# First block's mixing stage: the four q tiles first, the values between the k tiles; and the positions asked for before the bias tables

## The reference, cut to what matters

```python
h = _rmsnorm(x, mix_pre_g[l])
proj = h @ w_in[l]
qa, ka, va, qb, kb, vb, gate_a, gate_b = jnp.split(proj, splits, axis=-1)
ya = _neighbourhood_attention(qa.reshape(ha), ka.reshape(ha), va.reshape(ha), na_rpb[l]) @ w_branch_a[l]
...
s = jnp.einsum('brqhd,brkwhd->bhrqkw', qg, kg).astype(jnp.float32) * ATTN_SCALE
s = s + bias[None].astype(jnp.float32)
```

```python
inv_freq = jnp.power(jnp.float32(ROPE_THETA), -jnp.arange(0, dim, 2, dtype=jnp.float32) / dim)
ang = positions.astype(jnp.float32)[..., None] * inv_freq
```

## Time and profile before

| | |
|---|---|
| median of 3 runs | 3240.6 us (3239.19 to 3242.43) |
| the profiled execution's own time | 3239.51 us |
| its span in the profile | 3237.6 us |
| PE (TensorE matmul) busy | 3097.5 us, 96% of the span, 15386 matmuls |
| DVE busy | 1713.5 us, 53% |
| ACT busy | 1200.4 us, 37% |
| POOL busy | 292.5 us, 9% |
| mean TensorE clock granted | 0.986 of full |
| DMA | 339.65 MB, mean 105 GB/s |

### The profile page before, as it was taken

The page is one execution under the profiler, slowest core; times in us unless marked ns, Lnnn a source line. Parts: engine busy times, 40 slices in busy tenths (PEclk is TensorE's granted clock), DMA queues, the critical chain, the costliest instruction groups (busy, mean ns, idle before and its releaser), DMA issues.

```text
span 3237.6 us, 40494 instructions
## 1 busy us (share of the span) xinstructions
PE 3097.5 (96%) x15386; PEld 2514.2 (78%) x15386; DVE 1713.5 (53%) x3078; ACT 1200.4 (37%) x2229; POOL 292.5 (9%) x351
## 2 busy tenths in 40 slices
PE   7999989999999998999999999999999899999997
PEld 5888777788788887777768888887777767888886
DVE  5653354446555326655656555435656665555434
ACT  3322334443423233644542323223545453332222
POOL 2000110001100001111001100012111001100002
PEclk9999999999999998999999999999999999999998
DMA  4333373225232332224216222333323314323332
GB/s 148 109 98 115 99 143 111 92 88 175 86 104 93 115 98 71 96 88 149 74 40 189 97 98 92 102 106 117 94 85 107 126 43 146 124 92 103 95 96 91
DMA packets 107569, 339.65 MB, mean 105 GB/s; under 512 B 16608, under 2 KB 17136, under 8 KB 107248
## 3 DMA queue, kind: packets, MB, share of 16 engines
q1 hardware_dynamic: 86384, 273.90, 26.9%
q0 software_dynamic: 20992, 63.15, 6.5%
HBM read 300.55 MB, written 27.52 MB: 101 GB/s over the span
## 4 chain that ended last, share of the span: by engine, by line
PE 82%; ACT 6%; DVE 5%; issue 4%; DMA 2%; POOL 1%; SPq 0%; POOLq 0%; DVEq 0%; ACTq 0%
PE bk L1540 24%; PE bk L1542 24%; PE bk L1541 24%; ACT t L1760 2%; PE bk L1627 2%; PE bk L1605 2%; PE bk L1613 2%; PE bk L1577 1%; PE bk L1578 1%; PE bk L1579 1%; ACT t L1708 1%; ACT t L1768 1%; DVE t L1834 1%; PE bk L1590 1%; DMA t<-t 0%
## 5 line engine op out<-in xcount | busy, mean ns | idle before, releaser
L1540 PE MATMUL bk<-t,t 128*128 128x512 f32 x3808 | 1498.8, 394 | 67.9 <-DVE t L1834 27.1
L1542 PE MATMUL bk<-t,t 128*128 128x512 f32 x3808 | 1484.0, 390 | 0.0
L1541 PE MATMUL bk<-t,t 128*128 128x512 f32 x3808 | 1483.2, 389 | 0.0
L1540 PEld LDWEIGHTS bk<-t,t 128*128 128x128 f32 x3808 | 721.0, 189 | 239.1 <-issue 44.6
L1834 DVE TENSOR_TENSOR t<-t,t 128x1024 fp32r<-128x1024 f32 (+3 forms) x540 | 620.4, 1167 | 416.9 <-ACT t L1708 416.2
L1542 PEld LDWEIGHTS bk<-t,t 128*128 128x128 f32 x3808 | 720.4, 189 | 149.7
L1541 PEld LDWEIGHTS bk<-t,t 128*128 128x128 f32 x3808 | 721.5, 189 | 146.4 <-issue 1.7
L1708 ACT CAST t<-t 128x1024 fp32r<-128x1024 f32 (+3 forms) x540 | 513.5, 980 | 232.4 <-PE bk L1542 119.5
L1760 ACT ACTIVATE t<-t,t 128x256 f32<-128x256 f32 (+3 forms) x336 | 173.2, 516 | 140.8 <-DVE t L1911 140.0
L1751 ACT CAST t<-t 128x512 fp32r<-128x512 f32 x88 | 54.6, 621 | 441.7 <-DVE t L1898 441.7
L2141 POOL TENSOR_TENSOR t<-t,t 128x512 f32<-128x512 f32 x65 | 86.9, 1337 | 1428.9 <-ACT t L1738 1428.1
(11 more groups left out here) (165 smaller groups left out, 2035.1 us busy)
## 6 DMA issues: line engine op xcount, KB each, us to landing
t<-in_f_g SPq DMA_DIRECT2D x88, 512.0 KB, 4.3
t<-in_f_u SPq DMA_DIRECT2D x88, 512.0 KB, 3.6
t<-in_f_d SPq DMA_DIRECT2D x64, 512.0 KB, 4.4
t<-in_gate SPq DMA_DIRECT2D x48, 512.0 KB, 3.9
gate_scratch<-t POOLq DMA_DIRECT2D x64, 256.0 KB, 2.3
t<-gate_scratch POOLq DMA_DIRECT2D x64, 256.0 KB, 3.8
t<-in_f_d SPq DMA_DIRECT2D x32, 384.0 KB, 3.2
t<-in_wo SPq DMA_DIRECT2D x24, 512.0 KB, 3.8
```

Of the source, the lines that this page charges most:

```text
L1540: pe.matmul(o, wh, xh, start=start, stop=False)
L1541: pe.matmul(o, wh, xl, start=False, stop=False)
L1542: return pe.matmul(o, wl, xh, start=False, stop=stop)
```

## The change

Two edits. In the mixing stage the four q tiles are made first, in one `dense4` step; then k0 and k1; then the values with their store and their loads; then k2 and k3. In `rope_tables()` the load of the positions stands before the call of `bias_tables()`.

```diff
-        v_n = self.tokens_first("va", 512, 2, H, lambda t: vn[:, t, :], fr, by=lambda: (self.nv, self.nv_tok))
-        vst = self.load(D["values"].rearrange("(t p) c -> p t c", p=128), vn[:], v_n)
-        v_t = [[self.load(va[w][:, j, :],
-                          bass.AP(D["values"].tensor, (256 * j + WINDOWS[w]) * T, [[64 * T, 4], [T, 32], [1, T]]), fr, vst)
-                for j in range(2)] for w in range(4)]
         qt_, kt_ = [], []
         bt_ = {}
...
+        for m, r in enumerate(self.dense4([("qka", m) for m in range(4)], H)):
+            qt_.append(self.evacuate(OB, *r, qa[:, m, :].rearrange("p (t r c) -> p t r c", t=4, r=8), fr, view=by_columns))
         for m in range(4):
-            qt_.append(self.project("qka", m, H, qa[:, m, :].rearrange("p (t r c) -> p t r c", t=4, r=8), fr, view=by_columns))
-        for m in range(4):
+            if m == 2:
+                v_n = self.tokens_first("va", 512, 2, H, lambda t: vn[:, t, :], fr, by=lambda: (self.nv, self.nv_tok))
+                vst = self.load(D["values"].rearrange("(t p) c -> p t c", p=128), vn[:], v_n)
+                v_t = [[self.load(va[w][:, j, :],
+                                  bass.AP(D["values"].tensor, (256 * j + WINDOWS[w]) * T, [[64 * T, 4], [T, 32], [1, T]]),
+                                  fr, vst) for j in range(2)] for w in range(4)]
             kt_.append(self.project("qka", 4 + m, H, ka[:, m, :], fr))
             for kind in range(3) if m % 2 == 0 else ():
                 n = self.step("biased", bt=BT[:, kind, 2 * m:2 * m + 4, :], window=kind, t=bt_w)
...
+        a = self.load(pi_[:], D["positions"].partition_broadcast(128), self.now())
         self.bias_tables()
-        a = self.load(pi_[:], D["positions"].partition_broadcast(128), self.now())
```

## The result

| | changed kernel | before, on the same chip | ratio, 95% interval |
|---|---|---|---|
| first set | 3259.81 us median (3252.94 to 3262.26, 4 runs) | 3239.89 us (3238.0 to 3242.43, 4 runs) | 1.0056 [1.0043, 1.0068] |
| second set (an experiment below) | 3257.61 us (3249.61 to 3261.88, 6 runs) | 3243.41 us (3236.43 to 3249.52, 10 runs) | 1.0046 [1.0031, 1.0061] |

The changed kernel is slower, by 19.9 us in the first set and 14.2 us in the second; forecast were 13.7. The profile is of a run of 3258.6 us.

A forecast was written before the change was run, and what follows sets the result against it. PE carries 82% of the chain, so PE's standstills were taken to count. Positions -9.8 us and mixing stage +23.5 us gave +13.7 on 3239.5, 3253.2; with 1.1 us to the median, 3254 us, range 3244 to 3264.

The forecast's parts named there:

- The positions, -9.8 us: First FFN's start: loading positions earlier removes PE's stop, 7.3 us, and slow matmuls behind it, 2.45 us.
- third rival: Start-up: the positions' wait stays or another replaces it, leaving only +23.5 us, 3264 us; chance 0.05.
- B: Mixing stage: landing of the last bias load, which ends the wait of `biased` on DVE; taken as 455.5 us.
- first rival: Mixing stage: bias loads land before DVE wants them, so the kernel is faster, 3227 us; chance 0.08.
- The 1.6 us that the forecast took off for less weight traffic: Bias loads: one weight unit (0.52 MB) less beside them lets q0 move faster, landing them 1.6 us earlier.
- From B to the values, 11.3 us: Mixing stage: `biased`, a split, the `rstd` spreading and five evacuations hold PE's values until B + 11.3 us.
- From B to the attention, 46.4 us: Mixing stage: after the values begin, 2.4 us of slow start and 32.7 us of matmuls put the attention at B + 46.4.
- The stage, +23.5 us: Mixing stage, without the positions' gain: attention begins at 501.9 us instead of 478.4, 23.5 us later.
- The values in time: Attention: the stored values are loaded back before PE needs them, so no wait is counted there.
- second rival: Attention: the values return late and PE waits 12 us more, 3266 us; chance 0.06.
- The sum, +13.7 us: Whole kernel: +23.5 us from the mixing stage and -9.8 us from the positions, nothing counted behind the attention's start.
- -12 us where nothing else came in: Mixing stage: q tiles first remove the 8.30 us wait at `var` and its slow matmuls, if no wait is added.

The follow-up runs named there:

- experiment 1: The kernel before with only the positions' load moved ahead of the bias tables: 3232.2 us, ratio 0.9959 to the kernel before.
- experiment 2: The changed kernel with the positions' load put back behind the bias tables: 3267.92 us, ratio 1.0075 to the kernel before.
- experiment 3: The changed kernel with the first half of `biased` behind the values, the second staying behind k2: 3227.8 us, ratio 0.9949 to the kernel before.
- the last reordering: experiment 3 with the mixing stage's held-back evacuations run in forward order, q0's first: 3223.8 us, ratio 0.994 to the kernel before.

## Why the prediction was right

Its steps, each on the profile's own clock:

- **The positions, -9.8 us.** Measured at the mixing stage's first matmul are 7.4 us in the changed kernel's first profile, 9.4 in its second and 10.1 in experiment 1. Counted from the norm near 28 us, ahead of the positions' wait, they are 9.8, 9.8 and 9.9. The wait went, and nothing took its place: the third rival is out.
- **B, the landing of the last bias load.** Forecast as 455.5 us on the clock of before, 35.95 us after the first issue; measured 35.84 us. The first rival needed a landing at 441.8 us, 22.3 us after the first issue: out by 13.6 us. It needed loads that run at 150 GB/s; alone they ran at 116. The 1.6 us that the forecast took off for less weight traffic were sized well: from the first bias load's issue to the last one's landing q1 moved 2.19 MB before and 1.57 MB in the changed kernel.
- **From B to the values, 11.3 us.** 459.37 - 448.02 = 11.35.
- **From B to the attention, 46.4 us.** 493.94 - 448.02 = 45.9.
- **The stage, +23.5 us.** 103.5 - 80.6 = 22.9 in both profiles, 22.3 in experiment 2. The form was as described: one long stop in front of L1596, one of 4 us in front of L1578.
- **The values in time.** Nothing waited for their loads; the store, free of the bias loads in front of it, landed in 5.8 us. The second rival is out.
- **The sum, +13.7 us.** The terms give 22.9 - 9.8 = 13.1 at the attention, and so do the profiles once the start-up is taken off: 15.5 - 2.4 and 13.6 - 0.5. Behind that the prediction counted nothing, but some 2 us come back by the end of the mixing stage in both profiles (+15.5 to +13.6, and +13.6 to +11.5). They lie in the granted clock: from 260 to 280 us after the first scores it was 0.91 before (738.42 to 758.42 us) and 1.00 in both profiles of the changed kernel, 0.09 x 20 = 1.8 us. Before, it was 1.00 from 735 to 740 us and 0.79 from 740 to 745 us, where a stop of PE of 0.97 us ends at 740.77 us; the changed kernel stops for 1.02 and 0.85 us at the same matmul and keeps its clock. Why stays open.
- **The whole time.** The second set of runs has +14.2 us, the first +19.9; their intervals, 10 to 20 and 14 to 22 us, overlap, and 3.5 of the 5.7 us between them come from the runs of before. That 13.7 lies within 0.5 us of one of them is in part luck. The terms inside the stage are not: each was measured by itself.

The mechanism was right: the prediction named `biased` and what stood behind it as the cost, and gave the order alone a gain. What it did not say is that the +23.5 us hung on one placement that can be changed by itself; experiment 3 shows that with `biased` moved and the order kept the stage is 7.0 us shorter than before. Its two figures for the order without that wait, -12 us where nothing else came in and -4 us in the first rival, which counted a stop of 6.0 us and a slow start in front of the values, lie on either side of the -7.0 measured; that stop took 4.0 us.

## What to carry to other kernels

When work is moved past a step that waits for a DMA, list what now stands behind that wait on the same engine, and which engine waits for each of those instructions: here 27 us of PE hung on three adds whose first reader, the attention, came 42 us after them. Where such a step can't be fed earlier, put it behind everything that another engine is waiting for, and not merely later: one tile later won back 15.2 of the 29.9 us that the place behind the values did. And judge a change of half a per cent by a distance inside the stage that it touches, which repeated to 0.1 us here, while whole executions of one program differed by 9. Read it once more at a matmul well behind the stage, for what is won can be given back: the last reordering won 2.8 us up to the first scores and 1.1 up to the next norm.

## What I had not expected of the hardware

- A weight unit takes several times as long to land beside the bias loads. In the changed kernel three units of the values were issued from 412 us on, among the eight bias loads, and one of q and k after the last of those was down (DMA issues, KB each, median us to landing, windows 412 to 430 and 452 to 460 us):

```profile
t<-in_va SPq DMA_DIRECT2D x3, 512.0 KB, 16.1
```

```profile
t<-in_qka SPq DMA_DIRECT2D x1, 512.0 KB, 3.5
```

  One by one the three took 8.0, 16.1 and 21.4 us, each landing behind the one before; alone, a unit needs 3.5 us. While both queues had work they shared the engines evenly (q0 51.1% and q1 50.4% from 424 to 428 us). In experiment 3 a unit that was issued between 421 and 422 us, behind all bias loads, took 19.5 us. PE did not wait for any of these: the stops of the changed kernel came from `biased`, and experiment 3 has none between 427 us and the scores.
- Two executions of the changed kernel differ by 9.0 us in span (3256.8 and 3247.8 us), 7.6 us of it in the start-up and in one stretch of the layers, where the granted clocks differ. A single profile's end is therefore no measure of a change of this size.
